# A diagonal for each gathered row: the identity times the gate made ahead on ScalarE, then one scaling by the gelu

## The reference

```python
g = jax.nn.softmax(best_s, axis=-1)                      # the gates, 16 per head
u = u_tab[expert]
a = jax.nn.gelu(jnp.einsum('cd,chkd->chk', xc, u).astype(jnp.float32), approximate=False)
coeff = (g * a).astype(xc.dtype)
return jnp.einsum('chk,chkd->cd', coeff, v_tab[expert])
```

## Time and profile before

| what | value |
|---|---|
| runs, median (lowest to highest) | 4223.93 us (4222.44 to 4236.24) |
| the profiled execution's own time | 4242.59 us |
| its span in the profile | 4240.8 us |
| busy share of the span, PE / DVE / ACT / POOL | 78% / 51% / 31% / 37% |
| granted TensorE clock, mean | 0.926 |
| share of the 16 DMA engines' span taken by the gathers' queue | 66.9% |

### The profile page before, as it was taken

The page is one execution under the profiler, slowest core; times in us unless marked ns, Lnnn a source line. Parts: engine busy times, 40 slices in busy tenths (PEclk is TensorE's granted clock), DMA queues, the critical chain, the costliest instruction groups (busy, mean ns, idle before and its releaser), DMA issues.

```text
span 4240.8 us, 33463 instructions
## 1 busy us (share of the span) xinstructions
PE 3325.1 (78%) x9134; PEld 1565.7 (37%) x9134; DVE 2173.1 (51%) x4954; ACT 1296.3 (31%) x3390; POOL 1568.2 (37%) x1367
## 2 busy tenths in 40 slices
PE   8589989658776788878786887788778768976776
PEld 6545455323333454444332332233233223322222
DVE  0311122177567677667238447545744674485444
ACT  1011123111112343333133433433343343343333
POOL 0000000055544666667323344334423433344453
PEclk9899987789998999999898999999999999999999
DMA  7610031599988899989878899989989998999998
GB/s 283 237 39 22 22 114 56 183 354 386 330 298 311 329 360 382 340 316 372 353 250 309 339 371 373 361 331 377 377 327 362 369 374 337 373 380 368 379 381 327
DMA packets 283599, 1288.22 MB, mean 304 GB/s; under 512 B 27424, under 2 KB 52128, under 8 KB 192928
## 3 DMA queue, kind: packets, MB, share of 16 engines
q0 software_dynamic: 195120, 1073.83, 66.9%
q1 hardware_dynamic: 83696, 195.62, 12.6%
q10 hardware_dynamic: 4608, 16.78, 1.1%
HBM read 1243.13 MB, written 42.99 MB: 303 GB/s over the span
## 4 chain that ended last, share of the span: by engine, by line
DMA 22%; PE 16%; DVE 6%; ACT 4%; issue 4%; DVEq 0%; SPq 0%; POOLq 0%; ACTq 0%
DMA s_ring<-peer_uv,s_expert 15%; PE e_acc L405 11%; PE e_product L1635 5%; DMA e_more_slots<-peer_uv,s_expert 4%; DVE s_ring L331 2%; ACT s_diagonal L275 1%; DMA s_ring<-peer_v,s_expert 1%; ACT s_gate L288 1%; DMA s_x<-next_x 1%; DMA next_h<-e_work 1%; DMA e_work<-norm_ffn_row 1%; ACT s_dots L286 1%; ACT L286 0%; DVE e_work L1476 0%; DVE e_more_slots L331 0%
## 5 line engine op out<-in xcount | busy, mean ns | idle before, releaser
L405 PE MATMUL e_acc<-s_ring,s_diagonal 128*128 128x512 f32 x2676 | 1368.8, 639 | 497.3 <-ACT s_diagonal L275 406.0
L331 DVE CUSTOM_DVE_ANT_0 s_ring<-s_ring,s_x 128x1024 f32<-128x1024 f32 x886 | 1081.0, 1222 | 821.2 <-DMA s_ring<-peer_uv,s_expert 614.3
L244 POOL DMA_INDIRECT s_ring<-peer_uv,s_expert x555 | 656.7, 1183 | 1046.1 <-PE e_acc L405 667.8
L405 PEld LDWEIGHTS e_acc<-s_ring,s_diagonal 128*128 128x128 f32 x2676 | 499.1, 199 | 1313.0 <-ACT s_diagonal L275 745.5
L244 POOL DMA_INDIRECT s_ring<-peer_u,s_expert x331 | 368.2, 1113 | 392.4 <-DVE s_expert L1579 235.5
L286 ACT ACTIVATE s_dots<-s_dots 128x1 f32<-128x1 f32 x704 | 142.0, 202 | 1158.5 <-DVE s_dots L331 1157.6
L244 POOL DMA_INDIRECT s_ring<-peer_v,s_expert x327 | 369.3, 1129 | 336.1 <-PE e_acc L405 117.8
L275 ACT ACTIVATE s_diagonal<-s_ident,s_gate 128x128 f32<-128x128 f32 x1024 | 396.7, 398 | 291.3 <-PE e_acc L405 177.1
L405 PE MATMUL e_acc<-e_more_slots,s_diagonal 128*128 128x512 f32 x568 | 279.4, 615 | 75.9 <-ACT s_diagonal L275 73.5
L405 PE MATMUL a_acc<-s_ring,s_diagonal 128*128 128x512 f32 x426 | 247.4, 688 | 106.8 <-DMA s_ring<-peer_v,s_expert 47.2
L244 POOL DMA_INDIRECT e_more_slots<-peer_uv,s_expert x138 | 161.3, 1169 | 240.6 <-PE e_acc L405 183.1
(11 more groups left out here) (203 smaller groups left out, 3345.6 us busy)
## 6 DMA issues: line engine op xcount, KB each, us to landing
e_halves<-peer_scores SPq DMA_DIRECT2D x12, 2048.0 KB
e_halves<-mem_scores SPq DMA_DIRECT2D x6, 2048.0 KB
e_halves<-mem_values SPq DMA_DIRECT2D x6, 2048.0 KB
s_ring<-peer_uv,s_expert POOLq DMA_INDIRECT x555
p_w_in<-w_in SPq DMA_DIRECT2D x8, 1104.0 KB
f_w_big<-w_mem_kv SPq DMA_DIRECT2D x4, 2048.0 KB
f_w_big<-peer_w_q_t SPq DMA_DIRECT2D x2, 4096.0 KB, 17.8
peer_scores<-f_stage_s SPq DMA_DIRECT2D x16, 512.0 KB, 3.6
```

Of the source, the lines that this page charges most:

```text
L244: pool.indirect_dma_start(out=to, out_offset=None, in_=table, in_offset=bass.IndirectOffsetOnAxis(ap=self.expert[c % PICK_BUFFERS][:, k:k ...
L331: dve.tensor_tensor_reduce(row, row, self.x[:, :], 1.0, 0.0, ALU.mult, ALU.add, self.dots[:, k:k + 1]).then_inc(self.u_used, 1)
L405: last = pe.matmul(self.acc[:, at:at + BANK], self.diagonal[:, made % DIAGONALS, :], row[:, at:at + BANK], start=(n == group[0]), stop=(n ...
```

## The change

A new tile `e_gated` (128x128) is kept in the last stage. ACT's work on a pick from 320 on becomes: gelu in place; the diagonal, which is now `e_gated` times the gelu; and then, for the next pick, `e_gated` again, the identity times that pick's gate. The product of gelu and gate in one column is gone, and the gate is no longer written over. The three instructions per pick remain three. The wait for `gate_ready` moves with the new instruction, so it stands behind the pick before. Picks under 320 are not touched.

```diff
             if kind == "v":
+                made = self.pe_through[n]
                 if g >= ALONE_FROM:
-                    self.coeff_alone(g)
-                elif g % TOPK == 0 or n - 2 < self.stages[self.stage_of[n]][0]:
+                    self.diagonal_alone(g, made)
+                    continue
+                if g % TOPK == 0 or n - 2 < self.stages[self.stage_of[n]][0]:
                     act.wait_ge(self.coeff_ready, g // TOPK + 1)
-                made = self.pe_through[n]
...
-    def coeff_alone(self, g):
+    def gated_ident(self, g):
+        act = self.nc.scalar
+        c, k = divmod(g, PICKS)
+        if k % (2 * TOPK) == 0 or g == ALONE_FROM:
+            act.wait_ge(self.gate_ready, GROUPS * c + k // (2 * TOPK) + 1)
+        act.activation(self.gated[:, :], self.ident[:, :], ACT.Copy, scale=self.coeff(g)).then_inc(self.gated_ready, 1)
+
+    def diagonal_alone(self, g, made):
+
         act = self.nc.scalar
         c, k = divmod(g, PICKS)
         n = g - ALONE_FROM + 1
-        if k % (2 * TOPK) == 0 or n == 1:
-            act.wait_ge(self.gate_ready, GROUPS * c + k // (2 * TOPK) + 1)
+        if n == 1:
+            self.gated_ident(g)
         act.wait_ge(self.u_used, g + 1)
         act.activation(self.active[:, k:k + 1], self.dots[:, k:k + 1], ACT.Gelu).then_inc(self.activated_alone, 1)
+        act.wait_ge(self.gated_ready, n)
         act.wait_ge(self.activated_alone, n)
-        act.activation(self.coeff(g), self.active[:, k:k + 1], ACT.Copy, scale=self.coeff(g)).then_inc(self.coeff_made, 1)
-        act.wait_ge(self.coeff_made, n)
+        need(act, self.v_pe, made - DIAGONALS)
+        act.activation(self.diagonal[:, made % DIAGONALS, :], self.gated[:, :], ACT.Copy,
+                       scale=self.active[:, k:k + 1]).then_inc(self.diagonal_ready, 1)
+        if g + 1 < TOTAL_PICKS:
+            act.wait_ge(self.diagonal_ready, made)
+            self.gated_ident(g + 1)
```

More of the change, by code:

```diff
@@ L133, in __init__ @@
         self.more_slots = None
+        self.gated = None
         self.acc = None
@@ L141, in __init__ @@
         self.activated, self.coeff_ready, self.diagonal_ready = sem("s_activated"), sem("s_coeff_ready"), sem("s_diagonal_ready")
-        self.activated_alone, self.coeff_made = sem("s_activated_alone"), sem("s_coeff_made")
+        self.activated_alone, self.gated_ready = sem("s_activated_alone"), sem("s_gated_ready")
         self.h3_ready, self.flushed = sem("s_h3_ready"), sem("s_flushed")
@@ L1324, in pick_chunks @@
             stream.more_slots = sb("e_more_slots", [P, WIDE_RING - RING, D])
+            stream.gated = sb("e_gated", [P, P])
             mem_scores = sb("e_mem_scores", [P, DT, D])
```

## The result

| | median | lowest to highest | runs |
|---|---|---|---|
| before | 4228.25 us | 4222.44 to 4236.24 | 4 |
| the change | 4184.56 us | 4174.15 to 4193.24 | 4 |

The ratio is 0.9893, with a 95% interval of 0.987 to 0.9915: 1.1% faster, 44 us. In a second series with more runs it was 4182.12 us against 4230.34, 0.9887 (0.9862 to 0.9911). The forecast of 4214.4 us and its range (4190 to 4236) missed it. The first rival named 4184 us.

A forecast was written before the change was run, and what follows sets the result against it. The prediction took DMA bytes to bound the full stretches. Boundaries -6.5 us and full stretches -3 us summed to -9.5 us, from 4223.9 to 4214.4 us; range 4190 to 4236, the forecast's own 4206 to 4222.

The forecast's parts named there:

- The first rival: Full stretches: the ring's round, not the bytes, sets the pace; each round 0.33 us shorter, 4184 us; chance 0.17.
- the full stretches: Stretches from 2346 to 4216 us without boundaries, DMA share 0.98, about 1340 us; -3 us taken between 0 and -33.
- 2% hiccups: Idle DMA time in stretches at share 0.98: at most 27 us to win, a few filled by a longer line.
- The 3.0 us in line: Per ring round of 13.5 us, 10.5 us is needed; some 3.0 us are gathers standing behind other gathers.
- 99 rounds: Ring rounds of 13.5 us in about 1340 us of full-DMA time; each 0.33 us shorter would give -33 us.
- The gathers that wait for an earlier pick: Many visits end under 0.4 us of PE ahead of a gather, too short for a pick's four matmuls.
- POOL's phase: Gather issues take 0.94 us free, 1.94 just behind a dot's start; bounds -2 to +6 us at boundaries, taken as 0.
- The boundaries: Between chunks the waiting chain passes the product with the gate; -1.2 us per full boundary, -6.5 us in all.
- the costs on ACT: New copy and diagonal at 0.401 us each; ACT's 75 us more busy time covered by its wait for dots, costing nothing.
- the saving per pick: From dot to diagonal, removing the product with the gate saves 0.33 us, from 0.97 to 0.64 us.
- the gates' wait: ACT's wait for the gates moves one pick earlier; gates are complete before a chunk's first pick is gathered: 0.
- The last rival: At 79 places the new copy delays ACT's steps or DMA issues by 0.43 us; +27, 4251 us; chance 0.10.

The follow-up runs named there:

- e9: The complete changed kernel with two more ring pairs in the memory scores' table's tile from stream position 1640 on; 4153.48 us, ratio 0.9827.
- e2: The kernel before with four extra 128x128 copies on ScalarE between the product with the gate and the diagonal; 4360.15 us, ratio 1.0308.
- e7: The kernel before with one extra 128x128 copy on ScalarE behind the product with the gate; 4248.59 us, ratio 1.0046.
- e8: The changed kernel with a copy in place of the gelu from pick 320 on, so its table loads go; 4146.13 us, ratio 0.9811.
- e4: The changed kernel without the gelu and its table loads from pick 320 on, the diagonal scaled by the dot itself; 4117.29 us, ratio 0.973.
- e3: The changed kernel with one extra 128x128 copy on ScalarE between the gelu and the diagonal; 4206.66 us, ratio 0.9945.
- e10: The changed kernel itself, unaltered, measured and profiled again in a second series; 4182.12 us, ratio 0.9887.
- e5: The kernel before with a ring of 6 pairs instead of 5, the memory values' table left out for room; 4110.28 us, ratio 0.9705.
- e6: The changed kernel with a ring of 6 pairs, the memory values' table left out for room; 4090.70 us, ratio 0.9664.

## Why the prediction was wrong

**The step that failed is "the full stretches".** I took -3 us there between ends of 0 and -33, because a DMA share of 0.98 "leaves at most 2%" and 3.0 us of each round were spent in line. Both readings were wrong.

*The share.* It counts the time that packets take, and behind an idle time packets take longer. The DMA view of the kernel before, one microsecond behind the standstill of the earlier trace rows, has 22 packets of 8 KB, the first in 5 us. Together they count as 94.2% of 16 engines' time: 15.1 us, 685 ns each, at 180 GB/s. The last packets ahead of the idle time took 309 ns.

```profile
DMA packets 22, 0.18 MB, mean 180 GB/s; under 512 B 0, under 2 KB 0, under 8 KB 0
...
q0 software_dynamic: 22, 0.18, 94.2%
```

In the last chunk of the kernel before, q0 has 98.0% with 9298 packets, 1036 of them small: 0.980 x 16 x 178 us / 8262 = 338 ns. In the changed kernel it is 1.004 x 16 x 178 / 8988 = 318 ns, the small ones' time neglected in both.

```profile
DMA packets 9305, 67.76 MB, mean 381 GB/s; under 512 B 1036, under 2 KB 1036, under 8 KB 1036
...
q0 software_dynamic: 9298, 67.69, 98.0%
```

```profile
DMA packets 10116, 73.71 MB, mean 414 GB/s; under 512 B 1121, under 2 KB 1121, under 8 KB 1121
...
q0 software_dynamic: 10109, 73.63, 100.4%
```

Most packets of the steady state take 309 to 312 ns, eight to an engine and pick: the floor of 2.47 us. Packets of 8 KB over 400 ns are 6.5% of them in the last chunk before, 1.1% in the changed kernel, and 0.1% in e9. The "2% hiccups" were 10% of the pace, hidden in these longer packets. That the engines had run dry one by one is how I read this; what starts a hiccup is open.

*The 3.0 us in line.* I took 10.5 us of work from a round of 5 x 2.70 us. But 2.70 us was itself the pace of a line that was too short. Against the floor a round is 5 x 2.47 = 12.4 us, and of that 10.5, or up to 11.5 where POOL is held by a dot: 0.9 to 1.9 us of slack, spent by every hiccup. The slopes are of this size: +1.22 us cost 132 us (e2), +0.20 cost 18 (e7), -0.28 gave 29 (e8 to e4), each within a tenth or so of 99 rounds of it. Only e3 is off: 0.15 us more than the change cost 22 us where 99 rounds are 15. That the fit is so close is partly luck: the 99 rounds count the last chunk's 25, where e7 and e4 against e8 changed 1.6 and 0.1 us, and leave out the rounds behind the boundaries.

*The gathers that wait for an earlier pick.* Against the first rival I also held that a gather often starts less than 0.4 us behind a diagonal and so waits for an earlier pick. It does: the gather at 4041.89, shown above, starts 0.35 us behind the diagonal of one pick and was released by PE's end with the pick before. But that pick's diagonal comes earlier by the same 0.28 us, so this was no argument.

Measured, the term put at -3 is -32 to -41 us: 25 to 26 in the last chunk and 5 to 17 in the halves of the other four that don't stand behind a boundary, by the two profiles of the changed kernel.

**POOL's phase** I had with its size (0.94 and 1.94 us) and took at 0, "the shift having no preferred side", and as covered in the full stretches. It had a side. Where nothing disturbs the pace, a gather follows a dot at a fixed distance, in the last chunk's medians 2.23 us from dot to diagonal and 2.84 from there to the gather: 5.07 us, and two dots are 4.97. The kernel before sat 0.1 us behind a dot's start, the changed one 0.2 us ahead of it (4.79). But only a third of the kernel before's issues fell there, 43 of the last chunk's 128 within 0.2 us behind a dot's start; the mean over all 128 was 1.31 us against 0.95. In the last chunk, 25 of the 49 us between the profiles, the mean round went from 14.14 to 13.20 us: 0.27 less from dot to diagonal, 0.36 less of issue, 0.26 less from the issue's end to the dot, 0.05 in the rest. So the phase gave a little more than the saved instruction did, and not its full 1.0 us in each round.

**The boundaries**: -6.5 us expected, 1.2 each. The halves behind a boundary gave 12.5 us between the two profiles, 3.1 each, and 18.9 with e10's; with six pairs e5 to e6 gave 14.2 there. The chain that I counted passes five products with the gate per boundary; it doesn't show that rows behind a boundary also run with an empty line, where each round is shorter too. That this is the whole of the rest was not tried.

**Right were**: the costs on ACT (401 ns, 402 ns, the wait for dots as cover; the 75 us more of ACT's busy time cost nothing that a run shows), the saving per pick but for 0.05 us, and the saying that the gates' wait costs nothing. The last rival, ACT's steps delayed at 79 places by the copy, did not come; its 0.43 us was not tried alone. One cover is thinner than I wrote: back to back, dots start 1.15 us apart in the kernel before (3232.91 and 3234.06) and not 1.22, and ACT's three instructions take 1.11.

The first rival was worked out as 4184 us, with the right mechanism and the wrong weight, 0.17. That it met the median to the microsecond is luck: it was reckoned from a median of 4223.9 where the series had 4228, took 0.33 us a round for 0.28, and gave the last chunk's 25 rounds 8 us where they gave 25. Against it I had held the 0.98. The Trainium skill (HBM Reference, Specifications) has a core that streams alone at about 425 GB/s, bounded by its 16 DMA engines; I said that the trace disagreed. e9 moves 421 GB/s, near that figure: the trace had not disagreed, it had not been at its limit. On the other place that I cited from the Trainium skill (GPSIMD Engine Reference, section 8, Key points) the trace agrees, 0.94 against 1.94 us, and it was worth more than I gave it.

## What to carry to other kernels

Take the floor of a ring from the best stretches of the trace (dots 2.48 us apart), not from its mean, and measure the slack of a round against that floor; a share of DMA time near 1 with GB/s that differ from one stretch to another (378, 414, 421 at 0.98 to 1.01) was here a queue that ran dry, not a full one. If one more buffer is possible, it tells the two apart in one run. Where a short ring runs steadily, look at which instruction starts within 0.1 us of which: in the last chunk here 0.13 us less from dot to diagonal (2.23 to 2.10) gave 23 us, and the next 0.43 us gave 2.

## What was not expected of the hardware

Whether a gather's issue on POOL is held by the dot on DVE hangs on a few hundredths of a microsecond. Over the 12 traces, from pick 331 on, all 351 issues that started 0.01 to 0.10 us ahead of a dot's start took 0.93 to 0.99 us, though the dot ran beside them. All that started 0.05 to 0.20 us behind it took 1.83 to 1.99 us. Between these (0.01 ahead to 0.05 behind) both occurred. An issue that starts anywhere from 0.05 to 1.1 us behind the dot's start, 2333 of them, ends 0.81 us after the dot's end, with one exception (0.99).

A copy of 128x128 on ScalarE with no wait for the instruction ahead cost only 0.15 us behind a gelu and 0.20 us behind the product with the gate, against 0.33 us where it waits: overlap with its predecessor takes the rest.
